# State of an SSM chunk as three rounded products, with the decay mask product moved ahead of the state's addition

## What is computed

```python
decay = jnp.exp(jnp.where(causal, seg, -jnp.inf))
cb = jnp.einsum('bcign,bcjgn->bcijg', Cg, Bg)
y_diag = jnp.einsum('bcijg,bcijge,bcjgep->bcigep', cb, decay, xdt)
decay_to_end = jnp.exp(a_cum[:, :, -1:] - a_cum)
chunk_states = jnp.einsum('bcjgn,bcjge,bcjgep->bcgepn', Bg, decay_to_end, xdt)
...
def step(s, inp):
    st, dec = inp
    return s * dec[..., None, None] + st, s
```

## Time and profile before

| | us |
|---|---|
| runs shown, lowest / median / highest of 3 | 955.08 / 955.59 / 1718.46 |
| profiled execution | 955.14 |
| its span, first to last instruction | 953.3 |
| TensorE matmul busy in it | 933.8 (98%) |
| VectorE busy | 576.7 (60%) |
| ScalarE busy | 479.9 (50%) |
| GpSimd busy | 323.3 (34%) |
| granted TensorE clock, mean | 0.999 |

### The profile page before, as it was taken

How to read it: one execution, slowest core, us unless ns; L and a number is a source line. 1 busy time by engine, 2 the same in 40 slices (tenths; PEclk the granted TensorE clock), 3 DMA queues, 4 the chain that set the end, 5 groups by cost and what they waited for, 6 DMA issues and landing times.

```text
span 953.3 us, 18522 instructions
## 1 busy us (share of the span) xinstructions
PE 933.8 (98%) x7276; PEld 876.1 (92%) x7276; DVE 576.7 (60%) x1444; ACT 479.9 (50%) x947; POOL 323.3 (34%) x257
## 2 busy tenths in 40 slices
PE   9999999999999999999999999999999999999998
PEld 7998999999998999989998889998899988998787
DVE  4235522554235621466698589856898568986782
ACT  6335713464235613376437665346562565526852
POOL 2442244233341244225624242522344223442500
PEclk9999999999999999999999999999999999999999
DMA  7522232432234221211534815247143562327303
GB/s 213 182 75 68 72 106 73 123 121 89 70 93 153 89 89 52 89 24 45 150 94 119 226 47 167 90 138 220 49 144 91 159 199 78 125 84 218 104 12 106
DMA packets 144615, 105.92 MB, mean 111 GB/s; under 512 B 10754, under 2 KB 135860, under 8 KB 144464
## 3 DMA queue, kind: packets, MB, share of 16 engines
q1 hardware_dynamic: 134536, 100.19, 34.9%
q10 hardware_dynamic: 9992, 4.54, 1.9%
HBM read 91.99 MB, written 16.79 MB: 114 GB/s over the span
## 4 chain that ended last, share of the span: by engine, by line
PE 85%; DVE 9%; issue 2%; ACT 2%; DMA 1%; POOL 1%; SPq 0%; DVEq 0%; ACTq 0%; POOLq 0%
PE pp L1298 21%; PE pp L1300 21%; PE pp L1299 21%; PE pS L1408 2%; PE pO L1640 2%; PE pO L1636 2%; PE pT_ L1626 2%; DVE s_in L2355 1%; PE pO L1587 1%; PE pS L1559 1%; PE pO L1463 1%; PE pO L1462 1%; PE pp L1350 1%; PE pS L1597 1%; PE pT_ L1432 1%
## 5 line engine op out<-in xcount | busy, mean ns | idle before, releaser
L711 POOL TENSOR_TENSOR w_lo_buf<-w_raw_buf,w_hi_buf 128x512 fp32r<-128x512 f32 x214 | 279.1, 1336 | 470.2 <-ACT w_hi_buf L787 285.3
L1298 PE MATMUL pp<-h_hi,w_hi_buf 128*128 128x280 f32 (+2 forms) x1248 | 375.8, 301 | 1.6 <-issue 1.6
L1300 PE MATMUL pp<-h_hi,w_lo_buf 128*128 128x280 f32 (+2 forms) x1248 | 362.7, 291 | 0.0
L1299 PE MATMUL pp<-h_lo,w_hi_buf 128*128 128x280 f32 (+2 forms) x1248 | 362.1, 290 | 0.0
L1298 PEld LDWEIGHTS pp<-h_hi,w_hi_buf 128*128 128x128 f32 x1248 | 234.8, 188 | 10.0 <-issue 7.8
L1299 PEld LDWEIGHTS pp<-h_lo,w_hi_buf 128*128 128x128 f32 x1248 | 234.9, 188 | 4.2 <-issue 3.3
L1300 PEld LDWEIGHTS pp<-h_hi,w_lo_buf 128*128 128x128 f32 x1248 | 235.1, 188 | 0.0
L787 ACT ACTIVATE w_hi_buf<-w_raw_buf 128x2048 fp32r<-128x2048 f32 (+1 forms) x55 | 104.2, 1894 | 49.3 <-DMA w_raw_buf<-in_w_ssm_in 31.5
L1826 DVE TENSOR_TENSOR x<-x,pp 128x272 f32<-128x272 f32 (+2 forms) x120 | 53.0, 442 | 78.1 <-PE pp L1300 77.3
L1298 PE MATMUL pp<-og_hi,w_hi_buf 128*128 128x280 f32 (+2 forms) x256 | 75.1, 293 | 2.8 <-DVE x L1826 1.7
L1300 PE MATMUL pp<-og_hi,w_lo_buf 128*128 128x280 f32 (+2 forms) x256 | 74.4, 291 | 0.0
(11 more groups left out here) (372 smaller groups left out, 1644.5 us busy)
## 6 DMA issues: line engine op xcount, KB each, us to landing
w_raw_buf<-in_w_attn_in SPq DMA_DIRECT2D x16, 1024.0 KB, 5.3
w_raw_buf<-in_w_ssm_in SPq DMA_DIRECT2D x16, 1024.0 KB, 6.0
w_raw_buf<-in_w_attn_out SPq DMA_DIRECT2D x8, 1024.0 KB, 5.2
s_in<-in_state_ssm SPq DMA_DIRECT2D x32, 256.0 KB, 4.2
out<-s_in SPq DMA_DIRECT2D x32, 256.0 KB, 3.4
w_raw_buf<-in_w_ssm_out SPq DMA_DIRECT2D x8, 1024.0 KB, 6.6
seg<-a_scratch SPq DMA_DIRECT2D x12, 512.0 KB, 5.3
w_raw_buf<-in_w_attn_in SPq DMA_DIRECT2D x8, 512.0 KB, 6.3
```

The lines of the kernel that those rows point to most:

```text
L711: ins = pool.tensor_tensor(low_buf(n)[:, piece], raw[n % RAW_SLOTS][:, piece], high_buf(n)[:, piece].bitcast(F32), ALU.subtract)
L1298: pe.matmul(dst, hi[:, k, cols], a_hi[:, k, tk], start=(k == 0), stop=False)
L1299: pe.matmul(dst, hi[:, k, cols], a_lo[:, k, tk], start=False, stop=False)
L1300: mm = pe.matmul(dst, lo[:, k, cols], a_hi[:, k, tk], start=False, stop=(k == depth - 1))
```

## The change

For the full chunks (u = 2 to 5) the state's product becomes three products of float32r halves. `btok` is rounded and its low half made by VectorE in `prepare`; `xw` is rounded by ScalarE in a new `high_xw` at the end of each iteration u = 2 to 5, and its low half is made in place by VectorE in a new `low_xw`. TensorE waits on `xw_low` before the three products. `mix` moves ahead of `new_state` (and, at g = 3, u = 5, ahead of `gate_y`), and `low_xw` stands directly behind `new_state`. No buffer is added; the new tiles lie over `btok`, `xw`, `cv0` and `sT1`. The 16-token chunk keeps the old product.

```diff
+        btok_hi = at("btok_hi", [P, 2, P], F32R, offset=where["btok"])
+        xw_lo = at("xw_lo", [P, 2, WIDTH], F32R, offset=where["xw"])
+        xw_hi = at("xw_hi", [P, 2, WIDTH], F32R, offset=where["cv0"])
...
+        btok_lo = at("btok_lo", [P, 2, P], F32R, offset=where["sT1"])
...
+                def high_xw(u):
+                    v = UNITS * g + u
+                    act.wait_ge(xw_done, v + 1)
+                    act.wait_ge(b_done, v - 1)
+                    act.activation(xw_hi[:, v % 2, :], xw[:, v % 2, :], ACT.Copy).then_inc(xw_high, 1)
...
                         if u == 5:
                             start_decay(4)
                         start_decay(u)
+                    high_xw(u)
                     if (g, u) == (GROUPS - 1, 2):
                         silu_z(z_order(s)[0:HEADS])
                         exp_tables()
...
-                pe.matmul(pO[:, 0, :], btok[0:n, v % 2, :], xw[0:n, v % 2, :], start=True, stop=True).then_inc(b_done, 1)
+                if c == 0:
+                    pe.matmul(pO[:, 0, :], btok[0:n, v % 2, :], xw[0:n, v % 2, :],
+                              start=True, stop=True).then_inc(b_done, 1)
+                    return
+                pe.wait_ge(xw_low, 4 * g + u - 1)
+                pe.matmul(pO[:, 0, :], btok_hi[:, v % 2, :], xw_hi[:, v % 2, :], start=True, stop=False)
+                pe.matmul(pO[:, 0, :], btok_hi[:, v % 2, :], xw_lo[:, v % 2, :], start=False, stop=False)
+                pe.matmul(pO[:, 0, :], btok_lo[:, v % 2, :], xw_hi[:, v % 2, :],
+                          start=False, stop=True).then_inc(b_done, 1)
...
-                dve.tensor_copy(btok[0:n, b, :], pS[0:n, 0, P:2 * P])
+                if c:
+                    link(dve.tensor_copy(btok_hi[:, b, :], pS[:, 0, P:2 * P]))
+                    dve.tensor_tensor(btok_lo[:, b, :], pS[:, 0, P:2 * P], btok_hi[:, b, :].bitcast(F32), ALU.subtract)
+                else:
+                    dve.tensor_copy(btok[0:n, b, :], pS[0:n, 0, P:2 * P])
...
+            def low_xw(g, u):
+
+                v = UNITS * g + u
+                dve.wait_ge(xw_high, 4 * g + u - 1)
+                dve.tensor_tensor(xw_lo[:, v % 2, :], xw[:, v % 2, :], xw_hi[:, v % 2, :].bitcast(F32),
+                                  ALU.subtract).then_inc(xw_low, 1)
...
                     prepare(g, u)
+                    mix(g, u)
                     if (g, u) == (GROUPS - 1, UNITS - 1):
                         gate_y(g, 0)
                     new_state(g, u - 1)
-                    mix(g, u)
+                    low_xw(g, u)
```

More of the change, by code:

```diff
@@ L376, in build @@
         tok_high, tok_low, pt_low = sem("tok_high"), sem("tok_low"), sem("pt_low")
+        xw_high, xw_low = sem("xw_high"), sem("xw_low")
         x_tr, x_ready, h_ready = sem("x_tr"), sem("x_ready"), sem("h_ready")
```

## The result

The changed kernel's median is 963.23 us over 6 runs (960.67 to 965.27), that of the kernel before, run beside it on the same chip, 956.31: a ratio of 1.0072 with the 95% interval [1.0044, 1.0100], slower by some 7 us. One of the six runs of the kernel before took 1718.46 us and stays out of the ratio; the median without it is 955.59. The profiled executions differ by 960.67 - 955.14 = 5.5 us; the forecast for that difference was 6.9.

A forecast was written before the change was run, and what follows sets the result against it. TensorE, busy 98% of the span, was taken as the bound, with VectorE nearly full in the scan. 955.1 + 3.3 (group 3) + 3.6 (groups 0 to 2) = 962.0 us, the 2.8 saved already inside both terms; range 955.4 to 967.2.

The forecast's parts named there:

- TensorE's product: State's product on TensorE: 0.86 us becomes 0.69, saving 0.17 us per unit, 2.8 us over 16.
- VectorE's and ScalarE's added work: VectorE gets 0.9 us more per unit, 14.6 in all; ScalarE gets 16 copies of 0.6 us, 9.6 in all.
- Group 3: At u = 2 ScalarE's copy waits for xw, delaying the mask, VectorE and TensorE: 3.3 us later, between 0.5 and 4.5.
- Groups 0 to 2: Port collisions at u = 4 and the ec wait at u = 5: 1.2 us later per group, 3.6 for three.
- `mix(4)` waits out a piece: Groups 0 to 2, VectorE: mix(4) waits for one GpSimd low-half piece and ends about 674.2 on group 1's clock.
- Where the loss shows: Groups 0 to 2: the second sum_y, already bound by VectorE, comes 0.9 to 1.5 us late.
- L2217 might slip ahead: End of groups 0 to 2: if L2217 runs ahead of its GpSimd piece, the second sum_y is 0.9 us late, the low end.
- L1636 of u = 5: Group 1, TensorE: starts at 685.85 behind VectorE's L2198, against 684.93 before, 0.9 us late.
- A saving that arrives whole: Rival: all 2.8 us of the cheaper product reach the end, giving 952.3 us; chance 0.10.
- a tail that is covered: Rival: in group 3 too, the earlier mix gives back TensorE's pauses and covers the wait, about 955.6 us; chance 0.10.
- Only the last group pays: Rival: port and ec wait stay in the slack of groups 0 to 2, 0.1 us late each; 958.7 us, chance 0.22.
- The waits that stay whole: Rival: stalls of u = 4 and u = 5 reach each group's end, 3 us for three groups; 967.4 us, chance 0.13.

The follow-up runs named there:

- the kernel with the read first: Changed kernel with yoff's read directly behind new_state, low_xw next, ScalarE's copies moved (group 3 u = 2 behind Silus, u = 5 between Exps): 954.69 us, 0.9988.
- the first experiment: Changed kernel, but at group 3, u = 2 ScalarE does the Silus and table loads before the new copy of xw: 960.85 us, ratio 1.0053 to the kernel before.
- the product alone: Kernel before with three rounded products, high half by high half, in place of the float32 one; no low halves, no ScalarE copy, old order: 953.96 us, 0.9987.
- all three moves: Changed kernel with ScalarE's copy behind the Silus (group 3, u = 2), its u = 5 copy ahead of the ec Exp, and low_xw behind add_skip: 966.64 us, 1.0111.

## Why the prediction was right

The time forecast was 962.0, the median is 963.2 and the profiled execution 960.7; sign and size are right, and the range held. The mechanism of group 3 was right; that of groups 0 to 2 was right in kind, but which groups paid and where was not, and part of the close total is luck.

- *TensorE's product.* Right in kind, a little too large: 0.155 us saved per unit in place of 0.17. In the changed kernel's chain the three stand at 663.08, 663.31 and 663.54 as pieces of 0.23, 0.23 and 0.25.
- *VectorE's and ScalarE's added work.* 13.9 and 9.0 us against 14.6 and 9.6. As forecast, its size didn't decide: the kernel with the read first carries all of it at the time of the kernel before.
- *Group 3.* 3.37 us against 3.3, and each step of it (mask, `add_skip(2)`, `add_skip(4)`, L1648 of u = 5) within 0.3 us. The end value is closer than its parts, for small errors cancel: L1648 came 3.2 us late in place of 3.4, from there to `sum_y` 0.20 us were saved (0.17 forecast), and from `sum_y` to the last state transposes it took 0.35 us longer, which was not forecast. One row differs: the wait ahead of the first copy is 1.64 us, not 2.8, since `start_decay` itself ran 0.85 us later in its group (889.92 - 2.20 = 887.72 against 886.87 in the earlier trace rows). The copy ended at 892.81 - 2.20 = 890.6, 0.3 us ahead of the forecast, because it ends by `xw`. Moving it behind the Silus took 2.0 us off the last read, which makes this cause shown rather than argued.
- *Groups 0 to 2.* The sum, 2.8 us against 3.6, comes near by luck; its parts do not, and the first experiment's trace, with the same code in these groups, adds up to 5.9. The failing step is "`mix(4)` waits out a piece": that held in group 1 alone (in the first experiment's trace in groups 1 and 2). In groups 0 and 2 of the changed kernel `mix(4)` took the port 0.1 us ahead of GpSimd. I had read only group 1's rows closely and carried them over, when the whole question was a margin of 0.1 us, smaller than what my own shifts of 0.3 us were good for. The right form of this term was "0.4 or 1.8, by group".
- *Where the loss shows.* I put it at the second `sum_y`; it came at the first (1.02 to 1.17 us), and the second has no wait, since L2248 of part 1 now began at 697.83, in the same 0.01 us as GpSimd's piece, and took 0.33 us instead of the 1.40 of the earlier trace rows. The prediction's own aside, that L2217 might slip ahead, was the case. The chain ahead of it was right: `low_xw(5)` waited 1.01 us for the copy behind the `ec` Exp (1.3 forecast), and with the copy early the wait at `sum_y` is gone.
- *L1636 of u = 5.* Forecast 685.85; it came at 685.56 + 0.23 for the group's earlier start = 685.79. But it had no wait of its own: TensorE was late from u = 4, and VectorE's read, 684.33, was in time. A right number by the wrong release.
- *The rivals.* A saving that arrives whole and a tail that is covered are both refuted by +3.37 in group 3. "Only the last group pays" is wrong by group 1's 1.81, yet its condition (L711 behind `mix(4)`) is what happened in groups 0 and 2. The waits that stay whole would need 3 us in each of the three groups, and none lost more than 1.81.
- *Not forecast:* the 0.59 us gained ahead of the first scan, where the change touches nothing. The experiments' values there run from -1.11 to +2.01 (without the one profile with the disturbed attention part), so this is what one profiled execution scatters over 510 us. A single group scatters less where no operation changes its turn at the port (the product alone: three groups within 0.03 us), and by over 2 us where one does (group 2: +0.62 and +2.87).

Two readings of the prediction were wrong, without harm to the sum. It lets L1636 of u = 5 in group 3 wait for VectorE's read. In the kernel before it came straight behind the eight products by `seg`, and it was they that waited, for `mix`:

```profile
912.55 1.09 PE L1626 MATMUL pT_<-seg,xdt 128*64 128x128 f32 x16 [1.24 <-issue]
```

The read was over at 913.40, 0.18 us ahead of L1636, so this is worth no more than those 0.2 us. And in the stretch of the earlier trace rows VectorE had a second pause, 0.65 us in front of `new_state` at 679.53, where the prediction names the 0.86 us as the only one.

Open remains how much of the 8 us that the read first brings belongs to the read and how much to the two copies with it: moved alone they brought 1.8 and 3.0 us by the ratios (1.0072 to 1.0053 and 1.0041), intervals overlapping, and the three weren't run apart in every combination.

## What to carry to other kernels

Where a second engine feeds a saturated one, list what each iteration owes it in the order in which it asks, and put the feeder's operations in exactly that order: here the same work cost 7 us with the low half ahead of the read, 11 us with it a few operations too late, and nothing that can be told with the read first, the low half behind it and two of ScalarE's copies moved. A copy added to a third engine must be judged by what queues behind it while it waits for its input. And a float32 product of 512 columns as three rounded ones gains only 0.155 us of 0.86, so it pays where the halves can be made in idle time and not where the feeding engine is already late.

## What the runs showed of the hardware

**Half the clock behind a short wait.** In eight of the twelve edits' profiles TensorE ran at its lower level, 1.2 GHz, for some microseconds behind a short wait. Six of these lie in the scan or behind it: 2.34 us in the first experiment (clock 0.50, then 0.70), 2.19 us with the low half last (0.59, then 0.55), 2.18 with all three moves (0.63, then 0.52), 2.30 us with GpSimd later (0.65 over 4 us), 1.85 us with `gate_y` late, 1.48 us with the read first and GpSimd later (0.66, then 0.50); the last of these has another in the attention part, behind 2.94 us. Three lie ahead of the scan, behind a wait of 2.20 us near 507 us (copy of u = 5 early, all three moves, float32 in the last group; down to 0.50 or 0.54). The one with `gate_y` late, in 4 us stretches:

```profile
920.00:924.00 4.00, 2.64 (x15) 2.64 (x16) 2.73 (x8) 2.44 (x6) 0.00 (x0) 0.76 0.00 0
924.00:928.00 4.00, 4.00 (x27) 3.84 (x27) 2.42 (x7) 0.00 (x0) 0.00 (x0) 0.81 0.01 4
```

It isn't the wait's length alone. The same wait, without a fall of the clock in the kernel with the read first and with one in its copy with GpSimd later:

```profile
912.40 1.13 PE L1650 MATMUL pO<-bc,state 128*128 128x128 f32 x8 [1.49 <-DVE ec L2218]
```

```profile
920.13 1.59 PE L1650 MATMUL pO<-bc,state 128*128 128x128 f32 x8 [1.48 <-DVE ec L2218]
```

The changed kernel waited 2.70 us at 919.00 and kept its full clock (1.00 from 908 to 932), the kernel with the copy of u = 5 early 2.33 us at 918.39, and in the kernel with the low half last two more waits of 2.18 and 2.19 us passed without a fall. What decides between these cases isn't shown. Where it can be read off, the fall cost beyond the wait 3.02 - 1.65 = 1.4 us (first experiment), 10.34 - 9.17 = 1.2 us (GpSimd later) and, from L1650 to `sum_y` in the pair above, 2.66 - 1.67 = 1.0 us. That a stall of 2 us can cost 3.4 I had in no term.

**Who takes the port first.** A start 0.1 us ahead of GpSimd or 0.2 us behind it was worth 1.24 or 2.20 us to the same operation, and 0.33 or 1.40 us to a sum of 160 columns (in all three groups alike). GpSimd's `decay_state` takes the port as its low halves do. A shift of a few tenths of a microsecond elsewhere flips it, so such operations' times are to be carried as two values and not as a mean.
